# Router products moved inside the out projection, first weight splits moved ahead of the routing's exponentials, one buffer per tile in the final pass

## The chip, the cores and the metric

The kernel runs on one core of one Trainium2 chip. The metric is the device time of one execution in microseconds (us); it is given as the median of several runs. The work is spread over five instruction streams that run side by side and wait for each other through semaphores: TensorE (PE; its weight loads are PEld), VectorE (DVE), ScalarE (ACT), GpSimd (POOL) and SyncE (SP), which here only issues DMA transfers. ACT and POOL issue DMA transfers too. Each of the three issuers has a DMA queue of its own (SP's is q1, ACT's is q10, POOL's is q0), and all three are served by the same 16 DMA engines.

## The reference

The program is one layer of a decoder on 1024 prompt positions and 8 x 8 sample positions, 1088 tokens of width 1024, in float32. What the change touches is its second half:

```python
def branch_merge(x, a_out, b_out, ga, gb, w_proj_a, w_proj_b, w_out):
    m = jax.nn.sigmoid(ga) * (a_out @ w_proj_a) + jax.nn.sigmoid(gb) * (b_out @ w_proj_b)
    return x + m @ w_out

def channel_mix(h, norm_g, w_gr, b_gr, w_er, b_er, w_gate, w_up, w_down):
    xn = rmsnorm(h, norm_g).reshape(b * s, d)
    lg = (xn @ w_gr) + b_gr                       # 4 expert groups
    grp = argmax(lg); p_grp = softmax(lg)[grp]
    le = (xn @ w_er)[grp] + b_er                  # 8 experts of that group
    top_v, top_i = top_k(le, 2)
    wt = p_grp * softmax(top_v)
    eid = grp * 8 + top_i
    y = grouped_experts(xn, eid, wt, w_gate, w_up, w_down)
    return h + y

# grouped_experts: for each token's two experts e
#   hid = silu(x @ w_gate[e]) * (x @ w_up[e]);  y += wt * (hid @ w_down[e])
```

The first half (input projection, the spatial gate, the dilated attention of the prompt and the samples, and the key, value and gate-state outputs) comes before and is not changed.

## The kernel before

**Split products.** A float32 matrix product is made of three float32r products: each operand is split into a high part (a Copy on ACT that rounds to float32r) and a low part (a subtraction on DVE), and hi x hi, hi x lo and lo x hi are added up in PSUM. Every weight and every activation passes through ACT and then DVE before PE may use it.

**The out projection** goes over nine tiles of up to 128 tokens (`TORD` is their order, the sample tile of 64 tokens comes last). For each tile i PE runs, in this order: the first half of the product m @ w_out (512 columns, 24 matmuls), the eight transposes of the tile before (`h_transposes(i - 1)`, L1109), the second half (24 matmuls), the semaphore `out_mm`, and the router product of the tile before (`router(i - 1)`, L1119), which is true float32 and has 36 output columns. DVE takes the finished tile out of PSUM and adds x (L1931, semaphore `h_ready`), scales it (L1935, L1938) and reads the router's product (`logits`, L1869, semaphore `route_in`). ACT squares the tile (L1476), takes a root (L1480), copies the transposed tile out of PSUM for the router (`hT_evac`, L1466, semaphore `hT_ready`) and makes the high part of a coming tile (L1460). POOL stores the scaled tile to a scratch in HBM (L2186).

**The routing.** After seven tiles DVE runs `select(0, 7)` (the two best experts of each token; its end is the semaphore `assign`). PE then counts ranks (`ranks`, L1132 and L1133), transposes the last tile and runs its router product, which waits for `route_in` of the tile before. DVE runs `one_hot(0, 7)` (L1910 to L1913) between L1931 and L1935 of the last tile. At the end come `select(7, 9)`, the ranks, the table of tokens per expert (L1138) and its copies (L1947, L1948, semaphore `table_ready`). DVE then makes two differences (L1949, L1950, `rt_diff`), of which ACT takes exponentials (L1485, L1487).

**The experts.** There are 32 of them. Each has six weight chunks of 1 MB; `c_hi` on ACT (L1494) and `c_lo` on DVE (L2028) split a chunk, and six raw and three split buffers form rings. SP issues the first six chunk loads when `out_mm` has come nine times. POOL gathers the tokens of an expert by an indirect DMA (L2215 for the first three experts, L2201 for the rest), PE transposes them (L1190), ACT and DVE split them (L1498, L2034), and PE runs gate and up (L1201 to L1203), then down (L1224 to L1226). POOL scatters each result (an index copy L2206, then L2209) to a scratch. PE goes from expert to expert in an order written out by hand.

**The final pass** starts when all scatters have landed. For each tile SP loads both expert rows of each token (L774, 1 MB), DVE multiplies each by its weight and adds (L2093, L2094, semaphore `yo_ready`), and ACT issues the store (L1564, 512 KB, semaphores `y_out0` and `y_out1`). There are three load buffers and two result buffers, so DVE's tile t waits until the store of tile t - 2 has landed, and SP's load t waits for the sum of tile t - 3.

## Time and profile before

| | us |
|---|---|
| median of 3 runs | 1851.53 |
| lowest and highest | 1851.51, 1852.21 |
| profiled execution | 1851.12 |
| span of its records | 1849.2 |
| PE busy | 1741.3 (94% of the span) |
| DVE busy | 1011.6 |
| ACT busy | 775.5 |

The span is the time from the first to the last record of the profiled execution; 1.9 us of its own time lie outside. Times in the trace count from the span's start. The input projection and attention fill the first part, the out projection runs from about 1068 to 1190, the routing ends at 1208, the experts run from 1218 to 1799, and the final pass from 1804 to the end. In a timeline row the first number is the start, the second the time until the last instruction of the row ends, and the bracket tells how long the engine had been idle and what ended that.

### The profile page before, as it was taken

The numbers are of one execution on the slowest core, as the hardware profiler recorded it, in microseconds if no ns is written. First come the engines' busy times: TensorE is split into PE (matmuls) and PEld (weight loads), VectorE is DVE, ScalarE is ACT, GpSimd is POOL, SyncE is SP. The second block draws the span as 40 slices with busy tenths as digits, with TensorE's granted clock in tenths as the row PEclk, the third lists the DMA queues.
The fourth block names the chain that finished last, engine by engine and source line by source line (L and its number), as shares of the span: only waits on it lengthen the run. The fifth ranks groups of instructions, "written<-read, shape, count | busy, mean of one in ns | idle before, by whom it ended". The sixth has DMA issues, their size and how long they took to land.

```text
span 1849.2 us, 27970 instructions
## 1 busy us (share of the span) xinstructions
PE 1741.3 (94%) x11024; PEld 1562.1 (84%) x11032; DVE 1011.6 (55%) x1427; ACT 775.5 (42%) x1038; POOL 310.9 (17%) x341
## 2 busy tenths in 40 slices
PE   6999999999989999999999899969999999999980
PEld 5999988899979999988899888758888888888870
DVE  5104211277743333222356522469999898989964
ACT  5222111133333223222321222258777787877860
POOL 0001200000111112110101310003333232333310
PEclk9999999999989989999999999979999999999995
DMA  5322432121323223353563332369999999999957
GB/s 184 126 91 76 156 119 82 74 92 47 112 85 115 78 76 107 106 169 120 175 237 121 105 92 89 142 242 368 373 382 382 355 396 389 394 385 381 391 201 294
DMA packets 123930, 365.69 MB, mean 198 GB/s; under 512 B 20129, under 2 KB 80097, under 8 KB 97618
## 3 DMA queue, kind: packets, MB, share of 16 engines
q1 hardware_dynamic: 103250, 312.77, 46.4%
q0 software_dynamic: 19344, 46.99, 6.9%
q10 hardware_dynamic: 1232, 4.46, 0.6%
q8 instruction: 77, 1.26, 0.3%
q14 instruction: 27, 0.22, 0.0%
HBM read 330.41 MB, written 68.52 MB: 216 GB/s over the span
## 4 chain that ended last, share of the span: by engine, by line
PE 91%; DVE 4%; DMA 2%; ACT 1%; issue 1%; POOL 0%; SPq 0%; DVEq 0%; POOLq 0%; ACTq 0%
PE ps L800 15%; PE ps L801 15%; PE ps L802 15%; PE ps L1201 6%; PE ps L1203 6%; PE ps L1202 6%; PE ps L1226 3%; PE ps L1224 3%; PE ps L1225 3%; PE ps L1038 2%; PE ps L975 2%; PE ps L949 2%; PE ps L1190 1%; DVE part L2028 1%; DMA out_y_prompt<-part 1%; PE ps L1040 1%
## 5 line engine op out<-in xcount | busy, mean ns | idle before, releaser
L800 PE MATMUL ps<-part,part 128*128 128x256 f32 (+3 forms) x1912 | 610.9, 320 | 11.2 <-DVE part L1821 6.8
L801 PE MATMUL ps<-part,part 128*128 128x256 f32 (+3 forms) x1912 | 595.8, 312 | 0.0
L802 PE MATMUL ps<-part,part 128*128 128x256 f32 (+3 forms) x1912 | 595.5, 311 | 0.0
L2028 DVE TENSOR_TENSOR part<-part,part 128x2048 fp32r<-128x2048 f32 x192 | 438.8, 2292 | 57.4 <-ACT part L1494 52.9
L1494 ACT ACTIVATE part<-part 128x2048 fp32r<-128x2048 f32 x192 | 368.4, 1920 | 121.3 <-PE ps L1203 87.4
L800 PEld LDWEIGHTS ps<-part,part 128*128 128x128 f32 x1912 | 368.5, 193 | 20.0 <-DVE part L1821 8.5
L801 PEld LDWEIGHTS ps<-part,part 128*128 128x128 f32 x1912 | 368.8, 193 | 4.6
L802 PEld LDWEIGHTS ps<-part,part 128*128 128x128 f32 x1912 | 367.9, 192 | 5.3
L1201 PE MATMUL ps<-part,part 128*128 128x512 f32 x512 | 203.9, 398 | 5.1 <-DVE part L2034 4.1
L1203 PE MATMUL ps<-part,part 128*128 128x512 f32 x512 | 200.5, 392 | 0.0
L1202 PE MATMUL ps<-part,part 128*128 128x512 f32 x512 | 200.1, 391 | 0.0
L1576 DVE TENSOR_TENSOR part<-part,part 128x2048 fp32r<-128x2048 f32 x34 | 77.9, 2290 | 122.9 <-ACT part L1287 122.8
L1201 PEld LDWEIGHTS ps<-part,part 128*128 128x128 f32 x512 | 97.0, 189 | 26.7 <-DVE part L2034 4.7
L1203 PEld LDWEIGHTS ps<-part,part 128*128 128x128 f32 x512 | 96.5, 189 | 20.8
L1202 PEld LDWEIGHTS ps<-part,part 128*128 128x128 f32 x512 | 96.7, 189 | 19.0
L1224 PE MATMUL ps<-part,part 128*128 128x512 f32 x256 | 103.0, 402 | 1.9 <-DVE part L2042 1.9
L1358 ACT ACTIVATE part<-ps 128x384 f32<-128x384 f32 (+1 forms) x48 | 22.8, 474 | 186.9 <-PE ps L802 186.9
L1226 PE MATMUL ps<-part,part 128*128 128x512 f32 x256 | 100.8, 394 | 0.0
L1225 PE MATMUL ps<-part,part 128*128 128x512 f32 x256 | 100.6, 393 | 0.0
L1707 DVE TENSOR_REDUCE stat<-ps 128x4 f32<-128x512 f32 (+1 forms) x24 | 22.5, 936 | 121.0 <-PE ps L949 88.8
L2140 POOL DMA_DIRECT2D gate_scratch<-part x48 | 26.5, 552 | 342.3 <-ACT part L1358 342.3
L2201 POOL DMA_INDIRECT part<-xn_scratch,idxc x29 | 79.8, 2751 | 25.2 <-POOL idxc L2198 25.2
(241 smaller groups left out, 2032.3 us busy)
## 6 DMA issues: line engine op xcount, KB each, us to landing
part<-w_gate SPq DMA_DIRECT2D x64, 1024.0 KB, 8.1
part<-w_up SPq DMA_DIRECT2D x64, 1024.0 KB, 7.5
part<-w_down SPq DMA_DIRECT2D x64, 1024.0 KB, 7.4
part<-w_in SPq DMA_DIRECT2D x25, 1024.0 KB, 5.4
part<-x_prompt SPq DMA_DIRECT2D x16, 512.0 KB, 3.6
part<-expert_out_scratch SPq DMA_DIRECT2D x8, 1024.0 KB, 6.7
gate_scratch<-part POOLq DMA_DIRECT2D x32, 192.0 KB, 2.9
part<-gate_scratch SPq DMA_DIRECT2D x4, 1088.0 KB, 6.4
```

Of the source, the lines that this page charges most:

```text
L800: mm(out, lhs[0](k), rhs[0](k), start=(k == 0), stop=False)
L801: mm(out, lhs[0](k), rhs[1](k), start=False, stop=False)
L802: last = mm(out, lhs[1](k), rhs[0](k), start=False, stop=(k == n - 1))
L1201: mm(bank(2 + j % 2), xgh[:, kk, :], hi[:, k, :], start=(kk == 0), stop=False)
L1202: mm(bank(2 + j % 2), xgh[:, kk, :], lo[:, k, :], start=False, stop=False)
L1203: last = mm(bank(2 + j % 2), xgl[:, kk, :], hi[:, k, :], start=False, stop=(kk == KT - 1))
L1224: mm(bank(5 + half), hTh[:, kk, :], hi[:, k, cols], start=(kk == 0), stop=False)
L1225: mm(bank(5 + half), hTh[:, kk, :], lo[:, k, cols], start=False, stop=False)
L1226: last = mm(bank(5 + half), hTl[:, kk, :], hi[:, k, cols], start=False, stop=(kk == 3))
L1494: act_(ehi[:, off % NSPL, :], eraw[:, off % NRAW, :], ACT.Copy).then_inc(s("e_hi"), 1)
L2028: tt(elo[:, off % NSPL, :], eraw[:, off % NRAW, :], ehi[:, off % NSPL, :].bitcast(F32), ALU.subtract)\
L2201: pool.indirect_dma_start(xg, None, xn_d, bass.IndirectOffsetOnAxis(ap=idxc[:, 0:1], axis=0), bounds_check=T - 1, oob_is_err=False).then_i ...
```

## The change

Three parts. On PE the router product of the tile before moves from behind the second half of the out projection to its middle, after 12 of its 24 matmuls; `out_mm` now comes after both. On ACT the first three weight splits of the experts (`c_hi(0, 0)` to `c_hi(0, 2)`) move ahead of the routing's two exponentials and wait for `out_mm` instead of for the stores of the scaled tiles. In the final pass every tile gets its own buffer, in which the result overwrites the first of the two loaded rows; DVE no longer waits for a store, and SP keeps four loads ahead instead of three. Two semaphores (`masks_in`, `vn_out`) are made one, which changes no order.

On PE, at the end of the last tile of the out projection: L800 to L802 are matmuls of the second half, L1119 the router product of the tile before, L1133 and L1132 the ranks. Before:

```order
L800 MATMUL ps<-part_135,part_149 128x512
L801 MATMUL ps<-part_136,part_149 128x512
L802 MATMUL ps<-part_135,part_151 128x512
L1119 MATMUL ps<-part_144,part_156 128x36 [waits route_in,hT_ready]
L1119 MATMUL ps<-part_144,part_156 128x36 x7
L1133 MATMUL ps<-part_181,cbf 128x32 [waits assign]
```

Of the change, the same place (L1127 to L1129 are the out projection's matmuls, L1121 the router product, L1139 the ranks):

```order
L1127 MATMUL ps<-part_135,part_149 128x512
L1128 MATMUL ps<-part_136,part_149 128x512
L1129 MATMUL ps<-part_135,part_151 128x512
L1121 MATMUL ps<-part_144,part_156 128x36 [waits route_in,hT_ready]
L1121 MATMUL ps<-part_144,part_156 128x36 x7
L1127 MATMUL ps<-part_135,part_149 128x512
L1128 MATMUL ps<-part_136,part_149 128x512
L1129 MATMUL ps<-part_135,part_151 128x512
```

Twelve matmuls of the out projection now stand between the router product and the ranks; PE's work is the same in sum.

On ACT, from the last root of the out projection to the first gathered tokens: L1494 is the weight split, L1485 and L1487 the exponentials, L1498 the high part of the first expert's tokens. Before:

```order
L1480 ACTIVATE small<-small,cst 128x1 [waits act_own]
L1485 ACT_TABLE_LOAD
L1485 ACTIVATE part_158<-part_158 128x36 [waits rt_diff]
L1487 ACTIVATE part_172<-part_172 128x9 [waits rt_diff]
L1494 ACTIVATE part_199<-part_198 128x2048 [waits e_in0,x2_st1,x2_st0]
L1494 ACTIVATE part_199<-part_198 128x2048 [waits e_in1]
L1494 ACTIVATE part_199<-part_198 128x2048 [waits e_in2]
L1498 ACTIVATE part_202<-ps 128x1024 [waits xg_tr]
```

Of the change (L1486 is the root, L1501 and L1503 the exponentials, L1508 the tokens):

```order
L1486 ACTIVATE small<-small,cst 128x1 [waits act_own]
L1494 ACTIVATE part_199<-part_198 128x2048 [waits e_in0,out_mm]
L1494 ACTIVATE part_199<-part_198 128x2048 [waits e_in1]
L1494 ACTIVATE part_199<-part_198 128x2048 [waits e_in2]
L1501 ACT_TABLE_LOAD
L1501 ACTIVATE part_158<-part_158 128x36 [waits rt_diff]
L1503 ACTIVATE part_172<-part_172 128x9 [waits rt_diff]
L1508 ACTIVATE part_202<-ps 128x1024 [waits xg_tr]
```

The three splits no longer wait behind the exponentials. DVE's stream has no such move: its three subtractions still stand behind L1949 and L1950.

On DVE in the final pass, tiles 2 and 3. Before:

```order
L2093 SCALAR_TENSOR_TENSOR part_212<-part_211,wts,part_141 128x1024 [waits y_out0,yg_in2]
L2094 SCALAR_TENSOR_TENSOR part_212<-part_211,wts,part_212 128x1024 [waits dve_own]
L2093 SCALAR_TENSOR_TENSOR part_213<-part_209,wts,part_141 128x1024 [waits y_out1,yg_in0]
L2094 SCALAR_TENSOR_TENSOR part_213<-part_209,wts,part_213 128x1024 [waits dve_own]
```

Of the change:

```order
L2097 SCALAR_TENSOR_TENSOR part_211<-part_211,wts,part_141 128x1024 [waits yg_in2]
L2098 SCALAR_TENSOR_TENSOR part_211<-part_211,wts 128x1024 [waits dve_own]
L2097 SCALAR_TENSOR_TENSOR part_212<-part_212,wts,part_141 128x1024 [waits yg_in3]
L2098 SCALAR_TENSOR_TENSOR part_212<-part_212,wts 128x1024 [waits dve_own]
```

The waits for the stores (`y_out0`, `y_out1`) are gone; only those for the loads stay.

```diff
--- before.py
+++ after.py
@@ -358,9 +358,11 @@
     assert le_.at <= AFTER_W + 2 * D
     yb = Lay(AFTER_H).take(D)
 
+    YG = ("yg_in0", "yg_in1", "yg_in2", "yg_in3")
     lf = Lay(0)
-    yy = [lf.take(2, D) for _ in range(3)]
-    yo = [lf.take(D) for _ in range(2)]
+    yy = [lf.take(2, D) for _ in range(TILES)]
+    yo = [y[:, 0, :] for y in yy]
+    NYG = 4
 
     ps = ctx.enter_context(nc.psum_tensor("ps", [P, 8, 512], F32))
 
@@ -769,15 +771,15 @@
         sp.wait_ge(s("all_stored"), 1)
         for t in range(TILES):
             w = NSAMP if t == ST else P
-            if t >= 3:
-                sp.wait_ge(s("yo_ready"), t - 2)
-            dma(yy[t % 3][0:w, :, :], y_d.rearrange("(t j) d -> t j d", j=2)[col0(t):col0(t) + w]).then_inc(s(f"yg_in{t % 3}"), 16)
+            if t >= NYG:
+                sp.wait_ge(s("yo_ready"), t - NYG + 1)
+            dma(yy[t][0:w, :, :], y_d.rearrange("(t j) d -> t j d", j=2)[col0(t):col0(t) + w]).then_inc(s(YG[t % NYG]), 16)
 
         sp.wait_ge(s("cache_out"), 16 * len(pieces))
         for j in range(4):
             sp.wait_ge(s(f"k_st{j}"), 16 * kst[-1][j])
             sp.wait_ge(s(f"v_st{j}"), 16 * vst_n[-1][j])
-        sp.wait_ge(s("vn_out"), 16)
+        sp.wait_ge(s("masks_in_v_out"), 32)
         for j in range(2):
             sp.wait_ge(s(f"y_out{j}"), 16 * len(range(j, TILES, 2)))
 
@@ -1119,9 +1121,13 @@
                 last = mm(bank(6, RW), hTr[i % 2][:, k, :], wr[:, k, :], start=(k == 0), stop=(k == KT - 1))
             last.then_inc(s("rout_mm"), 1)
 
-        def out_half(i, half):
-            return three(bank(2 * (i % 2) + half), [lambda k, v=v: v[i % 2][:, k, :] for v in (mh, ml)],
-                         [lambda k, v=v: v[:, k, 512 * half:512 * half + 512] for v in wo], KT)
+        def out_part(i, half, k0, k1):
+            out, cols = bank(2 * (i % 2) + half), slice(512 * half, 512 * half + 512)
+            for k in range(k0, k1):
+                mm(out, mh[i % 2][:, k, :], wo[0][:, k, cols], start=(k == 0), stop=False, skip_group_check=True)
+                mm(out, mh[i % 2][:, k, :], wo[1][:, k, cols], start=False, stop=False, skip_group_check=True)
+                last = mm(out, ml[i % 2][:, k, :], wo[0][:, k, cols], start=False, stop=(k == KT - 1), skip_group_check=True)
+            return last
 
         ones, before_row = cbf[:, BONE:BONE + P], cbf[:, BLT:BLT + P]
 
@@ -1149,12 +1155,12 @@
                 last = three(bank(j // 2)[:, WB * (j % 2):WB * (j % 2) + WB], [lambda k, v=v: v[0][:, k, :] for v in (mh, ml)],
                              [lambda k, v=v: v[:, k, WB * j:WB * j + WB] for v in wo], KT)
             if i >= 1:
-                out_half(i, 0)
+                out_part(i, 0, 0, KT)
                 h_transposes(i - 1)
-                last = out_half(i, 1)
+                out_part(i, 1, 0, KT // 2)
+                router(i - 1)
+                last = out_part(i, 1, KT // 2, KT)
             last.then_inc(s("out_mm"), 1)
-            if i >= 1:
-                router(i - 1)
         pe.wait_ge(s("assign"), 1)
         ranks(0, NEARLY)
         h_transposes(TILES - 1)
@@ -1481,18 +1487,22 @@
             if t < TILES - 1:
                 hT_evac(t)
 
-        act.wait_ge(s("rt_diff"), 1)
-        act_(R["d4"], R["d4"], ACT.Exp).then_inc(s("rt_exp"), 1)
-        act.wait_ge(s("rt_diff"), 2)
-        act_(R["ex"], R["ex"], ACT.Exp).then_inc(s("rt_exp"), 1)
-
-
         def c_hi(b, off, first=False):
             act.wait_ge(s(f"e_in{off % NRAW}"), b * 16 + 16 * chunk_uses(off))
             if not first:
                 act.wait_ge(s("e_used"), b * 6 + (off - NSPL + 1))
             act_(ehi[:, off % NSPL, :], eraw[:, off % NRAW, :], ACT.Copy).then_inc(s("e_hi"), 1)
 
+        act.wait_ge(s("out_mm"), TILES)
+        for off in range(3):
+            c_hi(0, off, first=True)
+
+        act.wait_ge(s("rt_diff"), 1)
+        act_(R["d4"], R["d4"], ACT.Exp).then_inc(s("rt_exp"), 1)
+        act.wait_ge(s("rt_diff"), 2)
+        act_(R["ex"], R["ex"], ACT.Exp).then_inc(s("rt_exp"), 1)
+
+
         def xg_hi(b):
             act.wait_ge(s("xg_tr"), b + 1)
             act_(xgh, pair(0), ACT.Copy).then_inc(s("xg_hi"), 1)
@@ -1511,10 +1521,6 @@
                 act.wait_ge(s("y_st"), b * 16)
             act_(yb, flat(5)[:, 0:D], ACT.Copy).then_inc(s("y_read"), 1)
 
-        act.wait_ge(s("x2_st0"), 16 * 5)
-        act.wait_ge(s("x2_st1"), 16 * 4)
-        for off in range(3):
-            c_hi(0, off, first=True)
         xg_hi(0)
         c_hi(0, 3)
         c_hi(0, 4)
@@ -1558,9 +1564,9 @@
         for t in range(TILES):
             act.wait_ge(s("yo_ready"), t + 1)
             if t == ST:
-                dst, src = o["y_sample"].rearrange("b s d -> (b s) d"), yo[t % 2][0:NSAMP, :]
+                dst, src = o["y_sample"].rearrange("b s d -> (b s) d"), yo[t][0:NSAMP, :]
             else:
-                dst, src = o["y_prompt"][0, P * t:P * t + P, :], yo[t % 2]
+                dst, src = o["y_prompt"][0, P * t:P * t + P, :], yo[t]
             act.dma_start(dst, src).then_inc(s(f"y_out{t % 2}"), 16)
 
 
@@ -1667,7 +1673,7 @@
             elif un[0] == 6 and un[1] == 0:
                 vnorm(TILES - 1)
                 dve.wait_ge(s("const2_in"), 32)
-                dve.wait_ge(s("masks_in"), 16)
+                dve.wait_ge(s("masks_in_v_out"), 16)
             elif kind == "u":
                 if m == 0:
                     dve.wait_ge(s("ws_T"), 1)
@@ -2084,11 +2090,9 @@
                     hid_lo(b)
 
         for t in range(TILES):
-            dve.wait_ge(s(f"yg_in{t % 3}"), 16 * (t // 3 + 1))
-            if t >= 2:
-                dve.wait_ge(s(f"y_out{t % 2}"), 16 * (t // 2))
+            dve.wait_ge(s(YG[t % NYG]), 16 * (t // NYG + 1))
             w = NSAMP if t == ST else P
-            out, (ya, yc) = yo[t % 2][0:w, :], (yy[t % 3][0:w, j, :] for j in range(2))
+            out, (ya, yc) = yo[t][0:w, :], (yy[t][0:w, j, :] for j in range(2))
             i = TORD.index(t)
             own.then_wait(stt(out, ya, wts[0:w, i, 0:1], hbuf[0:w, t, :], ALU.mult, ALU.add))
             stt(out, yc, wts[0:w, i, 1:2], out, ALU.mult, ALU.add).then_inc(s("yo_ready"), 1)
@@ -2097,7 +2101,7 @@
     @block.gpsimd
     def _(pool):
         dma = nc.gpsimd.dma_start
-        dma(cbf[:, :], a["c_bf16"]).then_inc(s("masks_in"), 16)
+        dma(cbf[:, :], a["c_bf16"]).then_inc(s("masks_in_v_out"), 16)
 
         def window_store(kv, g, t, src, sm):
 
@@ -2119,7 +2123,7 @@
             window_store("v", g, t, vst[k % 4], f"v_st{k % 4}")
 
         pool.wait_ge(s("vn_ready"), TILES)
-        dma(o["state_sgu_v_sample"][0].rearrange("b t c -> (b t) c"), vn[0:NSAMP, ST, :]).then_inc(s("vn_out"), 16)
+        dma(o["state_sgu_v_sample"][0].rearrange("b t c -> (b t) c"), vn[0:NSAMP, ST, :]).then_inc(s("masks_in_v_out"), 16)
         for m in range(3 * AG):
             g, c = divmod(m, 3)
             c0, w = CHUNK[c]
```

## Rows read from the trace of the kernel before

**Rows 1.** Page: the chain that ended last, share of the span by engine

```profile
PE 91%; DVE 4%; DMA 2%; ACT 1%; issue 1%; POOL 0%; SPq 0%; DVEq 0%; POOLq 0%; ACTq 0%
```

**Rows 2.** Timeline of the final pass: start, length, instruction, idle before

```profile
1809.36 1.28 DVE L2093 SCALAR_TENSOR_TENSOR part<-part,wts,part 128x1024 f32<-128x1024 f32 x1 [17.74 <-DMA part<-expert_out_scratch]
...
1811.88 1.28 DVE L2093 SCALAR_TENSOR_TENSOR part<-part,wts,part 128x1024 f32<-128x1024 f32 x1
...
1845.76 0.55 ACTq L1564 DMA_DIRECT2D out_y_sample<-part  x1
```

**Rows 3.** Waits of DVE in the final pass, 1800 to 1850

```profile
DVE part L2093 <- DMA out_y_prompt<-part: 13.1, 6, 4.6
```

**Rows 4.** DMA queues, 1795 to 1850: packets, MB, share of 16 engines

```profile
q1 hardware_dynamic: 1232, 8.91, 45.3%
q10 hardware_dynamic: 1232, 4.46, 20.9%
```

**Rows 5.** Final pass by stretches: busy times, then PEclk, DMA share, GB/s

```profile
1807.00:1813.00 6.00, 0.00 (x0) 0.00 (x0) 3.61 (x3) 0.00 (x0) 0.00 (x0) 0.50 1.01 429
1815.00:1821.00 6.00, 0.00 (x0) 0.00 (x0) 1.90 (x2) 0.00 (x0) 0.00 (x0) 0.50 1.00 401
1825.00:1831.00 6.00, 0.00 (x0) 0.00 (x0) 2.85 (x3) 0.00 (x0) 0.00 (x0) 0.50 1.01 416
1840.00:1844.00 4.00, 0.00 (x0) 0.00 (x0) 3.73 (x4) 0.00 (x0) 0.00 (x0) 0.50 0.39 156
```

**Rows 6.** Timeline of one tile of the out projection

```profile
1165.31 0.25 DVE L1869 SCALAR_TENSOR_TENSOR lgt<-ps,small,part 128x36 f32<-128x36 f32 x1
...
1169.29 1.03 ACT L1466 ACTIVATE part<-ps 128x1024 f32<-128x1024 f32 x1 [5.41 <-PE ps L1109]
...
1174.58 1.87 PE L1119 MATMUL ps<-part,part 128*128 128x36 f32 x16
```

**Rows 7.** Timeline of the last tile and the routing

```profile
1185.37 0.39 DVE L1901 TENSOR_TENSOR part<-part,cst 128x224 bf16<-128x224 f32 x1
...
1188.18 1.87 PE L1119 MATMUL ps<-part,part 128*128 128x36 f32 x16
1188.38 1.23 DVE L1931 SCALAR_TENSOR_TENSOR part<-ps,part 128x1024 f32<-128x1024 f32 x1 [2.08 <-PE ps L802]
...
1190.78 0.68 DVE L1910 TENSOR_TENSOR part<-part,ps 128x224 f32<-128x224 f32 x2 [1.17 <-PE ps L1133]
...
1195.88 3.60 PE L1119 MATMUL ps<-part,part 128*128 128x36 f32 x16 [4.22 <-DVE lgt L1869]
```

**Rows 8.** Landing times of the first six chunk loads

```profile
DMA to landing us min/median/max: 4.9/10.8/16.3
```

**Rows 9.** Timeline from the table to the first expert's products

```profile
1209.30 1.08 POOL L2215 DMA_INDIRECT part<-xn_scratch,tabt  x1 [8.44 <-DVE tabt L1948]
1210.73 6.69 DVE L2028 TENSOR_TENSOR part<-part,part 128x2048 fp32r<-128x2048 f32 x3 [2.22 <-ACT part L1494]
1213.65 1.97 PE L1190 MATMUL ps<-cst,part 128*128 128x128 f32 x8 [5.76 <-DMA part<-xn_scratch,tabt]
1215.66 1.02 ACT L1498 ACTIVATE part<-ps 128x1024 fp32r<-128x1024 f32 x1 [1.46 <-PE ps L1190]
1217.35 1.22 DVE L2034 TENSOR_TENSOR part<-ps,part 128x1024 fp32r<-128x1024 f32 x1
1218.62 0.79 PE L1201 MATMUL ps<-part,part 128*128 128x512 f32 x1 [3.00 <-DVE part L2034]
```

**Rows 10.** A stretch as the experts start; columns as in rows 5

```profile
1220.00:1222.00 2.00, 2.00 (x6) 1.54 (x5) 0.00 (x0) 0.00 (x0) 0.00 (x0) 0.50 0.93 365
```

**Rows 11.** Timeline: GpSimd transfers that begin while VectorE subtracts

```profile
1216.42 1.89 POOL L2215 DMA_INDIRECT part<-xn_scratch,tabt  x1 [6.04 <-PE ps L1190]
...
1402.16 6.89 DVE L2028 TENSOR_TENSOR part<-part,part 128x2048 fp32r<-128x2048 f32 x3
1402.55 2.79 POOL L2209 DMA_INDIRECT expert_out_scratch<-part,idxy  x1 [2.14 <-issue]
```

**Rows 12.** Gathers of the expert loop: length in ns, min/median/max

```profile
L2201 POOL DMA_INDIRECT part<-xn_scratch,idxc x29: 2601/2734/2987, 1248.9 to 1750.8; - x29
```

## The prediction

> **What bounds the kernel now.** I read the page first: 91% of the chain that ended last runs through PE [rows 1]. So an edit counts only where PE works or waits on that chain, or where PE has already ended. I then read the timeline at the three edited places. In the out projection PE goes from tile to tile without a pause. Between 1190.8 and 1218.6 the chain leaves PE and runs through the routing [rows 7, 9]. After 1804.5 PE has nothing left to do. There DVE needs 1.28 us for each of two sums per tile, yet it waits 13.1 us in six waits for stores [rows 2, 3], and in that stretch the DMA engines fall to a share of 0.39 while DVE works off its last tiles [rows 5]. Neither DVE nor the DMA engines are full there; the two result buffers make them take turns.
>
> **Final pass.** Removed: DVE's waits for stores. Added: four loads ahead instead of three. The 13.1 us can't all be won, because loads and stores share the 16 DMA engines and 8.91 + 4.46 = 13.37 MB have to pass [rows 4]. Step by step with rows of before:
> - The first load lands at 1809.36 and the second before 1811.88 [rows 2]. At 429 GB/s [rows 5] a load of 1.05 MB takes 2.45 us, less than two sums (2.6 us), so the sums of tiles 0, 1 and 2 end at 1812.0, 1814.6 and 1817.2. The third load lands at about 1814.2.
> - From there a load and a store pass per tile, 1.57 MB. In mixed stretches the engines moved 401 and 416 GB/s at a share of 1.0 [rows 5]; I take 408, so 3.85 us per tile. Loads 3 to 7 land at 1818.1, 1821.9, 1825.8, 1829.6 and 1833.5, and the half-size load of the sample tile 1.9 us later, at 1835.4. Load t + 4 is issued at the sum of tile t, some four load times before its turn, so the queue never runs dry.
> - DVE ends tile 7 at 1836.1 and the sample tile at 1838.7. Before, the last store was issued at 1845.76 and the span ended 3.4 us later [rows 2]. That gives 1842.1, against 1849.2: -7.1 us.
> Bounds: if loads pass first and stores trail, the end goes by the bytes alone: 1.05 MB are through at 1809.36, the other 12.3 MB take 30.2 us at 408 GB/s, end near 1840, so -9. If the shared stretches run 10% slower, the 5.5 tile times grow by 0.4 us each, and if the last stores lag by another 1 us, it is -4. I take -7.0, nearest to the mixed rows.
>
> **Router products.** PE's work is the same: eight router products of 1.87 us [rows 6] change place. What hides them as before: the router product waits for ACT's copy of the transposes, which begins at 1169.29 as they end and takes 1.03 us, and it came at 1174.58 [rows 6]. Half of the second half (2.7 us) now lies behind it, so it comes at 1171.9, 2.6 us after the transposes, and 1.1 are needed. Its other wait is for DVE's read of the logits of the tile before, at 1165.31 [rows 6]; with the tile's end 1.9 us later that is 1167.2, still 4.7 us early. No gain, no loss for tiles 0 to 7. At the last tile the end of the products moves from 1188.2 to about 1190.1, and three things move with it. The ranks wait for `assign`, which DVE's L1901 gives at 1185.8 [rows 7]; it moves to 1187.6 and stays early. The ranks themselves end where they ended, since PE has done the same work by then. But DVE's L1931 now runs from 1190.25 to 1191.5, and L1910, which began at 1190.78, stands behind it: +0.7 us. Everything to the table follows: L1938, the logits, the last router product at 1195.88 [rows 7]. I take +0.7; bounds 0 and +1.87, the whole product. SP's chunk loads also start 1.9 us later. They landed 4.9 to 16.3 us after their issue, median 10.8 [rows 8], the first three thus by about 1200 and now 1202; ACT's splits end by 1204, before the exponentials can run (1209). The last of the six landed at about 1206 and now at 1208, before the first gather needs the engines. That costs nothing.
>
> **Weight splits ahead of the exponentials.** ACT's three splits leave the chain: DVE's first subtraction began at 1210.73 after 2.22 us idle, so the step before it, L1950, ended at 1208.5 [rows 9]. It can now begin right behind L1950, at 1208.5 + 0.7 = 1209.2, and the three end by 1216. But what is late next? DVE's L2034 at 1217.35 waited for two things: the third subtraction (1217.42) and ACT's L1498 (ended 1216.68) [rows 9]. So of the 2.2 us only 0.7 are on the path; beyond that the gather, the transposes and L1498 set it. The edit alone would bring -0.7, exactly what the last tile lost.
> And the gather now has company. Before, POOL's L2215 ran at 1209.30 for 1.08 us while DVE was idle [rows 9]. When POOL starts a transfer inside a subtraction of DVE it takes longer: the second gather took 1.89 us and ended 0.9 us after the subtraction beside it (1217.42); the store at 1402.55 began 0.39 us after the first of three subtractions and took 2.79 us, 0.9 us past the end of that first one (2.3 us each) [rows 11]; the 29 gathers of the loop, which begin inside a subtraction, take 2.73 us [rows 12]. So the first gather, ready at 1209.3 + 0.7 = 1210.0, would wait for the subtraction that ends at 1211.5 and end at 1212.4 instead of 1210.4. Transposes, L1498 and L2034 follow in their old distances: transposes 1215.7 to 1217.7, L1498 to 1218.7, L2034 to 1220.0, first product at 1220.1 against 1218.62 [rows 9]. Sum for routing and start of the experts: +1.5 us, both edits together. Bounds: +0.1 if the gather isn't held, and +6 if it is held behind all three subtractions (gather end 1216.9).
> The experts' loop is PE's all along, so the shift stays. PE starts it at the lower clock (granted 0.50, 1.2 GHz [rows 10]); whether the clock rises sooner or later after a later start can move the sum by up to 1 us either way, which I count in the range.
> The Trainium skill (SBUF — State Buffer, "Who interferes with whom") says that a VectorE instruction with two SBUF inputs holds up GpSimd's reads, but infers that such a subtraction does not stall the building of DMA descriptors. Here the measured 2.73 against 1.08 us decides against that inference [rows 9, 12]; by it the first gather would keep its 1.08 us, which is the first rival's case.
>
> **Sum.** -7.0 + 1.5 = -5.5 us on a span of 1849.2, so 1843.7, and 1845.6 for the profiled execution (1851.12 before). The median of the runs lies 0.4 us above that: 1851.53 - 5.5 = 1846.0.
>
> **Rivals.**
> - The gather is not held. For it: the form L2215 shows beside a subtraction only once, and there chunk loads were on the engines too. Against it: both longer transfers of rows 11 and the 29 of rows 12 end the same 0.9 us after the subtraction they began in. Table +0.7, gather end 1211.1, first product 1218.7: +0.1. Time 1851.5 - 7.0 + 0.1 = 1844.6.
> - The DMA engines take the place of the store waits. Loads run further ahead and slow the stores, or mixed traffic is slower when it never pauses. For it: in rows 5 the mixed stretches are already below the 429 of pure loads, and the two queues together took 66% of 55 us, 36.4 us of engine time, which packed without a gap from 1805 would end at 1841.4, and with tails later [rows 4]. Against: no share-1.0 stretch was under 400. Then -4 and +1.5: 1849.0.
> - The gather is held behind all three subtractions: +6 instead of +1.5, 1850.5. Against it: the store of rows 11 had three in a row ahead too and waited for one.
> - Slower than before: the router product inside the tile becomes a wait on every tile. It has 2.6 us of cover against 1.1 before ACT's copy is there; should ACT reach its copy later than now (it has a square, a root and a split of 1 us each in the same tile), PE stalls eight times. From 0.7 us per tile on, the kernel is slower than before; with 1 us each it is 1851.5 - 5.5 + 8 = 1854. Against it: ACT was idle for 5.41 us before that copy [rows 6].
>
> **Numbers.** Forecast 0.57 (own range 1844.9 to 1847.4), gather not held 0.17, DMA-bound final pass 0.16, gather held behind three 0.05, router stalls 0.05. 0.2% of the time is 3.7 us, about what a measurement here can tell from no change. Under 1847.8 lie nearly all of the first two and a fifth of the third: faster 0.77; same 0.18; slower 0.05. For 8 in 10: 1844.0 to 1849.2.
>
> **What would show it.** Final pass: no wait of L2097 for a store, sums about 3.9 us apart from tile 3 on, DMA share near 1.0 to 1838, last store issued near 1838.7 plus the shift. Routing: L1910's counterpart right behind L1931's, 0.7 us later than before. Start of the experts: the first gather about 2.3 to 2.4 us long with the subtraction beside it, DVE's L2034 waiting for ACT instead of for subtractions, first product 1.5 us later. The forecast is wrong if the final pass shrinks by less than 5.5 or more than 8.5 us, if PE waits in front of a router product, or if the shift at the first product of the experts is above 3 us.

## The result and the profile after

The changed kernel takes 1841.9 us (median of 7 runs, 1836.33 to 1846.07). The kernel before, beside it on the same chip, takes 1851.53 us (7 runs, 1844.13 to 1852.21). The ratio of the two times is 0.9951, with a 95% interval of 0.993 to 0.9973. I forecast 1846.0, in a range of 1844.0 to 1849.2: faster is right, but the time lies 2.1 us below the range. The profiled execution took 1836.33 us, with a span of 1834.4 (before: 1851.12 and 1849.2).

**Where the two profiles part.** The chain still runs through PE:

```profile
PE 91%; DVE 4%; DMA 3%; ACT 1%; issue 1%; POOL 0%; SPq 0%; DVEq 0%; POOLq 0%; ACTq 0%
```

I cut both spans at instructions that both have: the first transposes of the out projection (they come in its second tile), the first product of the ranks, the first expert product, the last one, and the first load of the final pass. Each number is a difference of two start times, the last one of a start and the span's end.

| Stage | before, us | after, us | difference |
|---|---|---|---|
| Start to the first transposes of the out projection | 1086.5 | 1078.5 | -8.0 |
| From there to the ranks | 103.41 | 103.54 | +0.1 |
| Ranks to first expert product | 28.74 | 29.79 | +1.05 |
| Experts, to the last down product | 580.04 | 579.40 | -0.6 |
| Last product to first final load | 5.83 | 5.84 | 0.0 |
| First final load to the end | 44.73 | 37.32 | -7.4 |

More than half of the difference between these two executions arises before the first edited instruction runs. In the first 1080 us nobody's work was changed; but TensorE was granted another clock (in these rows 1.00 is 2.4 GHz and 0.50 is 1.2 GHz). These are 600 to 700 us of before and then of after (columns as in [rows 5]: after the length come the busy times of PE, PE's weight loads, DVE, ACT and POOL, then granted clock, DMA share, GB/s):

```profile
600.00:700.00 100.00, 100.00 (x629) 93.31 (x628) 30.87 (x57) 27.10 (x101) 11.84 (x22) 0.90 0.23 76
```

```profile
600.00:700.00 100.00, 100.00 (x682) 92.85 (x681) 32.71 (x62) 29.05 (x110) 13.39 (x25) 0.97 0.25 82
```

PE counts as 100% busy in both. At 0.90 it gets through 629 products, at 0.97 through 682. Before has three stretches of 6.8 us at half clock in there, after has one.

**Final pass.** Timeline of after, to be held against [rows 2]:

```profile
1797.09 20.29 SPq L776 DMA_DIRECT2D part<-expert_out_scratch  x9
1801.93 1.28 DVE L2097 SCALAR_TENSOR_TENSOR part<-part,wts,part 128x1024 f32<-128x1024 f32 x1 [16.09 <-DMA part<-expert_out_scratch]
...
1810.58 1.28 DVE L2097 SCALAR_TENSOR_TENSOR part<-part,wts,part 128x1024 f32<-128x1024 f32 x1 [1.01 <-DMA part<-expert_out_scratch]
1814.28 1.28 DVE L2097 SCALAR_TENSOR_TENSOR part<-part,wts,part 128x1024 f32<-128x1024 f32 x1 [1.09 <-DMA part<-expert_out_scratch]
1818.01 1.28 DVE L2097 SCALAR_TENSOR_TENSOR part<-part,wts,part 128x1024 f32<-128x1024 f32 x1 [1.12 <-DMA part<-expert_out_scratch]
...
1830.95 0.55 ACTq L1570 DMA_DIRECT2D out_y_sample<-part  x1
```

And its stretches ([rows 5]):

```profile
1799.60:1805.60 6.00, 0.00 (x0) 0.00 (x0) 3.63 (x3) 0.00 (x0) 0.00 (x0) 0.50 1.01 426
1807.00:1813.00 6.00, 0.00 (x0) 0.00 (x0) 4.91 (x5) 0.00 (x0) 0.00 (x0) 0.50 1.00 391
1811.00:1825.00 14.00, 0.00 (x0) 0.00 (x0) 9.86 (x8) 0.00 (x0) 0.00 (x0) 0.50 1.01 424
1826.00:1831.00 5.00, 0.00 (x0) 0.00 (x0) 4.85 (x4) 0.00 (x0) 0.00 (x0) 0.50 0.95 371
```

DVE now waits for loads alone: not at all before its second and third tile, 1.0 to 1.1 us before each of the next four, 1.5 us before the last full one. Those in the middle are 3.7 us apart (1810.58, 1814.28, 1818.01). The DMA share is 1.01 in the middle and still 0.95 in the last 5 us before the last store is issued; before, it was 0.39 while DVE worked off its last tiles.

**Routing and start of the experts.** Timeline of after, against [rows 7, 9]:

```profile
1182.06 0.19 PE L1139 MATMUL ps<-part,cbf 128*128 128x32 bf16 x1
1182.25 1.22 DVE L1937 SCALAR_TENSOR_TENSOR part<-ps,part 128x1024 f32<-128x1024 f32 x1 [2.07 <-PE ps L1129]
1183.39 0.67 DVE L1916 TENSOR_TENSOR part<-part,ps 128x224 f32<-128x224 f32 x2
...
1201.04 6.69 DVE L2034 TENSOR_TENSOR part<-part,part 128x2048 fp32r<-128x2048 f32 x3
1201.90 2.37 POOL L2219 DMA_INDIRECT part<-xn_scratch,tabt  x1 [8.45 <-DVE tabt L1954]
1207.51 1.97 PE L1196 MATMUL ps<-cst,part 128*128 128x128 f32 x8 [7.01 <-DMA part<-xn_scratch,tabt]
1209.52 1.02 ACT L1508 ACTIVATE part<-ps 128x1024 fp32r<-128x1024 f32 x1 [8.11 <-PE ps L1196]
1210.57 1.22 DVE L2040 TENSOR_TENSOR part<-ps,part 128x1024 fp32r<-128x1024 f32 x1 [2.84 <-ACT part L1508]
1211.85 0.80 PE L1207 MATMUL ps<-part,part 128*128 128x512 f32 x1 [2.37 <-DVE part L2040]
```

The first of the three subtractions now starts before the gather and no longer behind it. L1916 follows L1937 with no idle time between them. The gather takes 2.37 us where it took 1.08, and DVE's L2040 now waits for ACT's L1508, as forecast. The count from the ranks: first expert product after 28.74 us before, after 29.79 now.

**Out projection.** One tile of after, against [rows 6]:

```profile
1161.33 1.02 ACT L1472 ACTIVATE part<-ps 128x1024 f32<-128x1024 f32 x1 [3.58 <-PE ps L1111]
...
1163.89 1.87 PE L1121 MATMUL ps<-part,part 128*128 128x36 f32 x16
```

The router product begins 2.56 us after ACT's copy of the transposes does, and the copy takes 1.02. It came 5.29 us after it before. The cover shrank as forecast, and it suffices.

### The profile page after: what moved, and what is told of

It reads as the page before. It is cut to its first block, busy times and chain, and to the rows that moved or that the text cites. A ratio compares the mean times of both kernels' runs of the same rounds, so it can differ in the third digit from the quotient of the medians.

```text
span 1834.4 us, 27971 instructions
## 1 busy us (share of the span) xinstructions
PE 1733.2 (94%) x11032; PEld 1554.6 (85%) x11032; DVE 1011.4 (55%) x1427; ACT 775.4 (42%) x1038; POOL 310.5 (17%) x341
## 4 chain that ended last, share of the span: by engine, by line
PE 91%; DVE 4%; DMA 3%; ACT 1%; issue 1%; POOL 0%; SPq 0%; DVEq 0%; POOLq 0%; ACTq 0%
PE ps L802 14%; PE ps L803 14%; PE ps L804 14%; PE ps L1207 6%; PE ps L1209 6%; PE ps L1208 6%; PE ps L1230 3%; PE ps L1232 3%; PE ps L1231 3%; PE ps L1040 2%; PE ps L951 2%; PE ps L977 2%; PE ps L1127 2%; PE ps L1129 2%; PE ps L1196 2%; PE ps L1128 2%
## 5 line engine op out<-in xcount | busy, mean ns | idle before, releaser
L802 PE MATMUL ps<-part,part 128*128 128x256 f32 (+2 forms) x1784 | 558.2, 313 | 11.3 <-DVE part L1827 6.9
L803 PE MATMUL ps<-part,part 128*128 128x256 f32 (+2 forms) x1784 | 544.8, 305 | 0.0
L804 PE MATMUL ps<-part,part 128*128 128x256 f32 (+2 forms) x1784 | 544.6, 305 | 0.0
L1494 ACT ACTIVATE part<-part 128x2048 fp32r<-128x2048 f32 x192 | 368.5, 1920 | 124.5 <-PE ps L1209 87.8
L802 PEld LDWEIGHTS ps<-part,part 128*128 128x128 f32 x1784 | 343.0, 192 | 15.6 <-DVE part L1827 8.6
L803 PEld LDWEIGHTS ps<-part,part 128*128 128x128 f32 x1784 | 343.2, 192 | 0.0
L804 PEld LDWEIGHTS ps<-part,part 128*128 128x128 f32 x1784 | 342.4, 192 | 0.0
L1207 PEld LDWEIGHTS ps<-part,part 128*128 128x128 f32 x512 | 97.2, 190 | 25.9 <-DVE part L2040 4.1
L1209 PEld LDWEIGHTS ps<-part,part 128*128 128x128 f32 x512 | 96.9, 189 | 20.8
L1208 PEld LDWEIGHTS ps<-part,part 128*128 128x128 f32 x512 | 97.1, 190 | 19.0
```

What stands on the lines that cost most here:

```text
L802: mm(out, lhs[0](k), rhs[0](k), start=(k == 0), stop=False)
L803: mm(out, lhs[0](k), rhs[1](k), start=False, stop=False)
L804: last = mm(out, lhs[1](k), rhs[0](k), start=False, stop=(k == n - 1))
L1207: mm(bank(2 + j % 2), xgh[:, kk, :], hi[:, k, :], start=(kk == 0), stop=False)
L1208: mm(bank(2 + j % 2), xgh[:, kk, :], lo[:, k, :], start=False, stop=False)
L1209: last = mm(bank(2 + j % 2), xgl[:, kk, :], hi[:, k, :], start=False, stop=(kk == KT - 1))
```

## The experiments

All the numbers "from the ranks" and "final pass" below are cut as in the table above. Each run was timed beside the kernel before on its own chip, and each ratio is the run's time over that of the kernel before beside it. In the code, `...` marks what is left out.

**before_copy: the same kernel once more.** No edit.

> The kernel before, unchanged, to see how far executions of one and the same kernel differ and where. Theory A (the part of the gain that was not forecast is a matter of TensorE's granted clock in the attention stage, which differs from execution to execution): the start of the out projection (L1109's first instruction, 1086.5 us in the trace of before, 1078.7 in that of the change) comes at another time here too, by 3.4 us for each stretch of 6.8 us at the lower clock that is more or fewer between 500 and 700 us, and the runs differ by 3 to 10 us among themselves. Rival B (the change itself made that stage faster): the out projection starts within 1 us of 1086.5 and the runs stay within 1 us of each other.

Measured: 1851.21 us (12 runs, 1843.59 to 1854.18), ratio 1.0008 (0.9994 to 1.0021). The kernel before, run 35 times beside it: median 1848.66, from 1842.91 to 1854.09. So one and the same kernel spreads over 11 us on this chip, twice what I forecast for the change. The spread goes with the clock: the 6 of the 35 runs with a mean granted clock of 0.965 took 1851.3 to 1854.1 us, the 5 with 0.972 took 1842.9 to 1843.8. The profile of this run is no witness for that: it again has three stretches at the lower clock between 600 and 700 us, and its first transposes start at 1086.2, within 1 us of the profile of before, as rival B would have it. A profile of unedited stages that differs comes with splits_only below. The row of this run:

```profile
600.00:700.00 100.00, 100.00 (x630) 93.31 (x629) 30.86 (x57) 27.10 (x101) 11.79 (x22) 0.90 0.23 76
```

**final_only: the final pass alone.** The change, with the router products at the tile's end and the splits behind the exponentials as before:

```diff
-    yy = [lf.take(2, D) for _ in range(3)]
-    yo = [lf.take(D) for _ in range(2)]
+    yy = [lf.take(2, D) for _ in range(TILES)]
+    yo = [y[:, 0, :] for y in yy]
 ...
```

> Before with the buffers of the final pass alone (router product at the tile's end, weight splits behind the exponentials). Theory A: from the first load of the final pass to the end of the span 37.3 us as in the change (44.7 before), so -7.4 us; first product of the experts 32.0 us after the last tile's L1109 begins, as before (1190.6 to 1218.6: 28.0 us from the transposes, unchanged within 0.3 us). In time about 1.1 us better than the whole change, -7 us against before, beside what the clock does. Rival B (the buffers bring what was forecast but the rest of the gain came with the other edits): here the time is 3 us or more above the change's.

Measured: 1842.29 us (12 runs), ratio 0.9968 (0.9952 to 0.9984). Final pass 37.26 us against 44.73, from the ranks to the first expert product 28.73, unchanged. By its stages this edit is the whole gain of the change; its ratio agrees, but is too coarse for the 1.1 us by which I expected it to beat the change.

**router_only: the router product in the middle, alone.**

```diff
-                last = out_half(i, 1)
+                out_part(i, 1, 0, KT // 2)
+                router(i - 1)
+                last = out_part(i, 1, KT // 2, KT)
 ...
```

> Before with only the router product moved into the middle of the tile's second half. Theory A: the first ranks product to L1910 grows from 0.90 to 1.33 us, and everything behind it to the first product of the experts follows, +0.4 us; PE does not wait in front of a router product. Time +0.4 us, not to be told from none. Rival B: this edit gives a part of the unforecast gain, so the time falls by 2 us or more, and the nine tiles of the out projection (first L1109 to last) take less than 104.1 us.

Measured: 1849.29 us (12 runs), ratio 1.0001 (0.9985 to 1.0016). Its profile:

```profile
1190.92 1.23 DVE L1935 SCALAR_TENSOR_TENSOR part<-ps,part 128x1024 f32<-128x1024 f32 x1 [2.08 <-PE ps L1127]
1192.06 0.68 DVE L1914 TENSOR_TENSOR part<-part,ps 128x224 f32<-128x224 f32 x2
```

L1914 comes right behind the long read of L1935, with no idle time; from the ranks the first expert product comes after 29.16 us instead of 28.74, so +0.43, and the out projection before them is 0.13 longer (103.54 against 103.41). PE waited for nobody from 1087 to 1192. The rival of a stall in every tile is refuted.

**splits_only: the weight splits ahead of the exponentials, alone.** The three `c_hi(0, off, first=True)` stand before the first `rt_diff` wait.

> Before with only the three weight splits of ACT moved ahead of the exponentials. Theory A: DVE's first subtraction begins right behind L1950, the first gather takes 2.4 instead of 1.1 us because it begins inside it, the transposes come 1.3 us later, and the first product of the experts comes +0.6 us against before (28.0 us after the last L1109 begins, now 28.6). Rival C (what the page on SBUF infers: such a subtraction doesn't hold up a GpSimd transfer, and the 2.37 us of the change had another cause): gather 1.1 us, first product 0.7 us earlier, 27.3 us. Rival B: the time falls by 2 us or more.

Measured: 1848.92 us (12 runs), ratio 0.9999 (0.9986 to 1.0013).

```profile
1201.21 2.29 DVE L2027 TENSOR_TENSOR part<-part,part 128x2048 fp32r<-128x2048 f32 x1
1202.08 2.37 POOL L2214 DMA_INDIRECT part<-xn_scratch,tabt  x1 [8.44 <-DVE tabt L1947]
```

The gather starts 0.87 us into the first subtraction and ends at 1204.45, 0.95 us after that subtraction (1203.50) though two more follow it. First expert product from the ranks: 29.26, +0.5 us by itself. The profile of this run took 1843.66 us although the edit gains nothing: it has one stretch at the lower clock between 600 and 700 us where before has three, and its first transposes start at 1079.3, 7.2 us earlier than in before, long ahead of anything that was edited. One profile against another would have credited the splits with 7.5 us.

**hold: the subtractions wait until POOL has issued the gather.** On the changed kernel:

```diff
+            if b == 0: pool.sem_inc(s("zeroed"), 1)
 ...
+        dve.wait_ge(s("zeroed"), 3)
         for off in range(3):
             c_lo(0, off)
```

> The change with DVE's first weight subtraction held until POOL has issued the first gather; nothing else differs. Theory A (the subtraction lengthens the gather): the gather takes 1.1 us instead of 2.37, and although all three subtractions begin 1.1 us later, the first product of the experts comes earlier, 29.0 us after the first ranks product instead of 29.8. Rival C (the gather's 2.37 us have another cause, such as ACT's splits or the queue): the gather stays near 2.4 us and the first product comes later, at 30 us or more.

Measured (one run, 1845.37 us, in which the first transposes started only at 1089.1):

```profile
1212.44 6.74 DVE L2034 TENSOR_TENSOR part<-part,part 128x2048 fp32r<-128x2048 f32 x3 [0.77 <-POOLq L2223]
1212.46 1.08 POOL L2220 DMA_INDIRECT part<-xn_scratch,tabt  x1 [8.44 <-POOLq L2223]
```

1.08 us again, and the first expert product 28.49 us after the ranks against 29.79 in the changed kernel: -1.3 us. So the early start of the subtractions is what lengthens the gather, and that is what the early splits cost. But look at the two starts: the gather is not alone here. The first subtraction begins 0.02 us before it and runs on for 1.2 us after it. A subtraction beside the gather does no harm; one that is already under way does. All 13 profiles of this study agree on that. In 400 of their indirect transfers (gathers and scatters, whose rows are given by numbers in a tile), the gather of the changed kernel among them, a subtraction of 128x2048 was running and had begun 0.19 us or more before: they took 1.88 to 3.01 us and ended 0.87 to 0.95 us after it. In 6 more it had begun within 0.02 us, and in another 231 it began up to 0.19 us later: they took 0.98 to 1.08 us.

**early_lo: the first subtraction even earlier.** On the final pass alone, `c_lo(0, 0)` ahead of the last tile's logits, the other two held until the gather has been issued.

> The change with the router product back at the tile's end, the first of DVE's three weight subtractions moved into its wait for the last router product, and the other two held until the first gather has been issued. Theory A: the first gather takes 1.1 us again, DVE's L2034 counterpart waits only for ACT's copy, and from the first ranks product to the first product of the experts it takes 28.1 us (before 28.7, the change 29.8). Together with the final pass the profile gives -8.0 us against before on equal clock stretches, 1.8 us under the change. Rival D (the lengths of the gather and of the start do not hang together): the gather is short but the start stays at 29 us or more.

```profile
1190.93 2.29 DVE L1881 TENSOR_TENSOR part<-part,part 128x2048 fp32r<-128x2048 f32 x1
...
1204.54 4.54 DVE L1881 TENSOR_TENSOR part<-part,part 128x2048 fp32r<-128x2048 f32 x2 [0.76 <-POOLq L2224]
1211.92 1.22 DVE L2041 TENSOR_TENSOR part<-ps,part 128x1024 fp32r<-128x1024 f32 x1 [2.84 <-ACT part L1508]
```

Measured: gather 1.08 us, first expert product after 28.04 us, 1.75 us earlier than the changed kernel. But the experts then took 580.53 us instead of 579.40, so 1.1 us of it are given back. That is the clock: within the experts TensorE had the lower clock for 8.3 us here and for 6.3 us in the changed kernel, while it was idle between products for the same 4.5 us in both. Time 1841.56 us (9 runs), ratio 0.9965 (0.9952 to 0.9977): the same as the changed kernel's, below.

**after_copy: the changed kernel once more, beside early_lo.** No edit.

> The change itself again, on the same chip as the version above. Theory A: by its stages it is 6.2 us faster than before (final pass -7.4, routing and start of the experts +1.05, out projection +0.15), so the median stands at a ratio of about 0.9966 to before when each side has many runs, and the runs spread over some 10 us; the start of the out projection lies at 1078.6, 1082.4 or 1086.3 us by whether there were one, two or three stretches at the lower clock between 600 and 700 us. Rival B (the change also made an untouched stage faster): the ratio stays at 0.995 or below and the out projection begins at 1078.5 again.

Measured: 1842.09 us (12 runs, 1836.17 to 1849.07), ratio 0.9965 (0.9951 to 0.9979), which on the 1849.13 us of the kernel before beside it (20 runs) is -6.5 us. Its profile has the stages of the changed kernel again: 29.69 us to the first expert product, final pass 36.96.

**look2buf and look3: what of the final pass does it.** look2buf keeps the new buffers and four loads ahead, and puts back the waits for stores; look3 keeps everything but has three loads ahead.

```diff
+            if t >= 2:
+                dve.wait_ge(s(f"y_out{t % 2}"), 16 * (t // 2))
```

```diff
-            if t >= NYG:
-                sp.wait_ge(s("yo_ready"), t - NYG + 1)
+            if t >= 3:
+                sp.wait_ge(s("yo_ready"), t - 2)
```

> The change's own buffers and four loads ahead, but DVE still waits in tile t for the store of tile t - 2, as before. It parts the two halves of the final edit. Theory A (the store waits made the length): from the first load to the end 43 us or more, near the 44.7 of before. Rival E (the deeper load queue or the separate buffers brought the gain): 40 us or less.

> The change with its own buffers, but SP keeps only three loads ahead, as before. Theory A (the store waits alone made the length): from the first load to the end 37.3 us within 0.5 us, since a load is still issued before the one in front has landed. Rival E (the fourth load ahead matters): 39 us or more.

Each was run once (1843.47 and 1839.83 us), so only their stages count. look2buf: final pass 44.67 us, as before the change (44.73), and the same sum of waits as [rows 3]:

```profile
DVE part L2099 <- DMA out_y_prompt<-part: 13.1, 5, 6.2
```

So the waits for stores hold the final pass at its length; the fourth load without taking them away brings 0.06 us. look3: 38.58 us, so without the waits, and still with three loads ahead, 6.1 of the 7.4 us are won, and the fourth load is worth the other 1.3. I had expected next to nothing, and the rival more; both missed. Its fourth tile waits longer for its load than in the changed kernel (1.87 us against 1.0 to 1.1):

```profile
1813.81 1.28 DVE L2097 SCALAR_TENSOR_TENSOR part<-part,wts,part 128x1024 f32<-128x1024 f32 x1 [1.87 <-DMA part<-expert_out_scratch]
```

I take it that the load queue then has too little behind it while stores take their share; that was not tried further.

**gate_only and gate_between: the clock.** What stands ahead of a stretch at the lower clock in the kernel before? The timeline of one attention slot:

```profile
627.90 0.60 PE L932 MATMUL ps<-cbf 128*128 128x512 bf16 x2
628.44 3.37 PE L949 MATMUL ps<-part,part 64*128 64x128 f32 x16
631.74 0.71 PE L959 MATMUL ps<-cst,part 128*128 128x128 f32 x4
632.24 3.52 PE L975 MATMUL ps<-part,part 128*128 128x64 f32 x16
635.52 0.61 PE L800 MATMUL ps<-part,part 128*128 128x320 f32 x1
635.94 0.47 PE L801 MATMUL ps<-part,part 128*128 128x320 f32 x1
```

```profile
632.00:639.00 7.00, 7.00 (x33) 7.00 (x32) 2.33 (x5) 1.93 (x8) 0.00 (x0) 0.51 0.13 37
```

The clock falls at 632.2 us. The gate products (L800, L801, 320 columns) take 0.61 and 0.47 us here and 0.31 at full clock. Ahead of them PE spends 7.3 us on the small products of attention (64 rows in L949, 64 columns in L975, with four transposes, L959, between them). But only the first 3.8 of these lie before the fall: L975 already runs at the lower clock, where the same 16 products take 3.52 us instead of 1.90. And the same group comes without a fall, 17 us earlier in the same profile:

```profile
611.21 3.37 PE L949 MATMUL ps<-part,part 64*128 64x128 f32 x16
614.51 0.66 PE L959 MATMUL ps<-cst,part 128*128 128x128 f32 x4
615.00 1.90 PE L975 MATMUL ps<-part,part 128*128 128x64 f32 x16
```

So the group takes 5.7 us at full clock, and it does not lead to the lower clock each time: of its four passes between 609 and 675 us the clock fell in three in before, in one in after. Both of the next kernels move the 24 gate products of each slot between the probabilities' transposes and the products with V, so that large products stand between the small ones: gate_only on the kernel before, gate_between on early_lo.

```diff
+            if 1 <= sl < NU + 2:
+                gate_mm(sl)
 ...
-            if 1 <= sl < NGU:
+            if NU + 2 <= sl < NGU:
                 gate_mm(sl)
```

> Before, with one move on PE in the attention stage, none of it part of the change: in each slot the 24 matmuls of a gate unit stand between the transposes and the value products of the prompt's attention instead of behind them. Theory A (the lower clock between 600 and 700 us comes from the 7.4 us of small attention products in a row, L949, L959 and L975, in front of it): no run of small products is longer than 4.1 us now, the 6.8 us stretches at the lower clock between 600 and 700 us are gone or one is left, the out projection begins at 1075 us or earlier instead of 1078 to 1087, and the runs spread over less than the 11 us of before. Rival F (the lower clock there has nothing to do with what PE does just before): one to four stretches stay and the start lies between 1078 and 1087.

> The same move on top of the version with early subtractions (label early_lo). Theory A: the stages of both add up: final pass 37.2 us, first ranks product to the experts' first product 28.0 us, out projection from 1075 us on; median 1834 us or less, a ratio of 0.992 or less to before. Rival F: median about 1841 us, as early_lo.

Measured: gate_only 1842.14 us (6 runs, 1840.22 to 1843.51), ratio 0.9955 (0.994 to 0.9971); gate_between 1833.92 us (6 runs, 1831.12 to 1836.31), ratio 0.9912 (0.9896 to 0.9928). The same 100 us, of gate_only and of gate_between:

```profile
600.00:700.00 100.00, 100.00 (x703) 94.48 (x701) 33.10 (x62) 29.54 (x111) 13.50 (x25) 0.98 0.25 83
```

```profile
600.00:700.00 100.00, 100.00 (x719) 94.18 (x719) 35.04 (x67) 30.19 (x117) 14.59 (x27) 1.00 0.26 87
```

gate_between keeps the full clock (2.4 GHz) through all of it. Its first transposes start at 1074.8 us, those of gate_only, with one stretch of 3.4 us left, at 1077.3, above the 1075 that I expected. The spread of the runs is 3.3 and 5.2 us (six runs each), against 10.0 in the ten runs of the kernel before beside them. gate_between beats both kernels of the study. What was moved is unchanged in size and number, so it is the order that counts: early_lo without the move had 0.9965 (0.9952 to 0.9977), which lies wholly above the interval of gate_between.

## Why the prediction was wrong, point by point

**Final pass, forecast -7.0: right.** Measured -7.4 (37.32 against 44.73, and -7.5 alone). Over all profiles it is a little more, -7.8: six with the waits for stores took 44.6 to 45.5 us, 44.9 on average, and six with the whole new final pass 36.8 to 37.3, 37.1 on average. The mechanism is the forecast one: no waits for stores, then loads one behind the other. Tiles came 3.7 us apart against 3.85, because mixed traffic moved 424 GB/s from 1811 to 1825 and not 408 (391 in the first mixed stretch, from 1807). The DMA-bound rival (-4) is refuted by final_only.

**Router products, forecast +0.7: right, measured +0.56** (+0.43 behind the ranks, +0.13 ahead of them). The mechanism is the forecast one: L1916 is queued behind the long read, and stands 1.33 us behind the ranks against 0.90. In the records it starts 0.08 us before L1937 ends, where I had put it right behind.

**Splits, forecast +0.8 on top of it: measured +0.5 alone and +0.6 beside the router product.** The subtractions leave the path, and the gather, held until the subtraction under way has ended, takes 2.37 us (forecast about 2.4). hold shows that their earlier start lengthens it. It is held for one subtraction, not for all three: the rival at +6 is refuted, and so is the one in which it isn't held. The prediction drew too wide a conclusion from this, though. The Trainium skill (SBUF — State Buffer, "Who interferes with whom") infers that such a subtraction does not stall descriptor building. For the indirect transfers of this kernel that fails, 2.37 against 1.08 us. For the direct transfers that POOL issues it holds in the same traces: 162 of them began 0.21 us or more inside such a subtraction and took 0.53 to 0.58 us all the same, the one of 233.75 us among them:

```profile
233.46 2.29 DVE L1576 TENSOR_TENSOR part<-part,part 128x2048 fp32r<-128x2048 f32 x1
233.75 0.55 POOL L2127 DMA_DIRECT2D a_scratch<-part  x1 [4.64 <-DVE part L1618]
```

An indirect transfer also reads its row numbers out of a tile (`tabt`, `idxc` or `idxy`); that this reading is what has to wait was not tested.

**Sum of the edits, forecast -5.5.** By stages it is -7.4 + 1.05 + 0.13 = -6.2 us, so the terms were right in kind and the sum 0.7 too small, half of it in the final pass. The experts' loop took 0.6 us less as well, but it varies that much without any edit to it (580.04 and 580.01 in two profiles of before, 579.62 in final_only, 579.41 in gate_only), and with the clock: the lower clock was granted in it for 7.5, 7.3, 6.7 and 6.3 us of these. That is the term which the prediction gave up to 1 us either way, and I credit none of it to the change. The loop is also why router_only and splits_only show no loss from the ranks to the last down product (608.77 and 608.72 us against 608.78). That is -6.2 to -6.8; by the ratio of after_copy -6.5 us (0.9951 to 0.9979, so -9.1 to -3.9). The seven runs of the result give more, 0.9951, but their interval reaches to 0.9973, so the two agree.

**The step that failed is the base, and with it the range.** I wrote that "the median of the runs lies 0.4 us above that: 1851.53 - 5.5 = 1846.0", and took three runs within 0.7 us of each other for the kernel's time. The seven runs beside the result have the same median, 1851.53, so this comparison alone does not show it. But over more runs the kernel before has medians of 1848.66 (35 runs), 1849.13 (20) and 1850.49 (10), and single runs from 1842.91 to 1855.37, while the changed kernel came out at 1841.9 and 1842.09. The base was 1.0 to 2.9 us too high, and that with the 0.7 to 1.3 us of the sum makes up 1.7 to 4.2 of the 4.1 us by which 1846.0 missed. The range counted only the unknown costs of the edited places, and "up to 1 us either way" for the clock at the start of the experts. It held nothing for a stage that the change doesn't touch: the clock in attention was put at nothing. Of the 9.6 us between the medians, 6.2 to 6.8 are the change's. The rest, some 3 us, is chance in which executions were timed. That they differ by how long TensorE had the lower clock is shown by the mean granted clock of the runs (in the changed kernel 0.973 at 1836.33 and 1837.27 us, 0.967 at 1844.26 to 1846.07); that the stretches between 600 and 700 us are what differs is seen in the profiles alone. There half clock for 6.8 us takes 3.4 us of work from TensorE, and the starts of the first transposes line up by the number of stretches, from none to four 3.6 us for each on average:

| Profile | stretches of 6.8 us, 600 to 700 | first transposes of the out projection start, us |
|---|---|---|
| gate_between | none | 1074.8 |
| after, look2buf, splits_only, after_copy | 1 | 1078.5, 1078.5, 1079.3, 1079.4 |
| early_lo, final_only | 2 | 1081.8, 1082.3 |
| before_copy, before, router_only | 3 | 1086.2, 1086.5, 1087.2 |
| hold | 4 | 1089.1 |

look3 has one stretch here and starts at 1080.9; its granted clock in the first 200 us is 0.97, where that of the changed kernel is 1.00. So such stretches also happen elsewhere. Why the same program draws one in one execution and three in another is not settled. That the small products lead to them rests on the order of the rows and on gate_only and gate_between, against the passes of the same group without a fall; I did not test the small products by themselves, and the cause of the lower clock stays open.

With hindsight: had I forecast the change from typical medians (1848.7 to 1850.5) with the same -5.5, I would have said 1843.2 to 1845.0, and with a spread of 3 us either side for the clock the range would have held the result.

## What to carry to other kernels

Before a gain is forecast, look at whether the kernel's own executions agree: cut the profile at instructions that two executions share, and ask whether the untouched stages have the same length and the same granted clock. A range needs that spread beside the unknowns of the edits. And where an engine waits for stores out of a few buffers, the wait's sum is no forecast of the gain: work out instead when the transfers, packed without a pause, would be through.

## What the runs showed of the hardware

- An indirect transfer that GpSimd begins 0.19 us or more after a VectorE subtraction of 128x2048 began takes 1.88 to 3.01 us and ends 0.87 to 0.95 us after it (400 of them in 13 profiles). One that begins within 0.02 us of the subtraction, or just ahead of it, takes 0.98 to 1.08 us though the subtraction runs beside it. Direct transfers of GpSimd are not held: 0.53 to 0.58 us inside such a subtraction.
- Loads and stores on two queues together moved 424 GB/s over 14 us at a share of 1.01, nearly as much as loads alone (426), after 391 in the first mixed stretch.
- TensorE can be 100% busy and still be granted half its clock for 6.8 us. In the kernel before it fell in three of four passes through the same small products (64 rows, then 64 columns, 5.7 us at full clock), in the changed one in one of four. Putting large products between the small ones took 0.45% off the kernel before (ratio 0.994 to 0.9971) and left its work as it was.
